# Output weights by column halves, and the tail of the first ring of expert chunks reordered

## The reference, cut to what matters

```python
x = x + merged @ w['w_out']                       # 1024 x 1024
hn = rms_norm(x, w['norm_ffn_g'])
x = x + hier_moe(hn, ...)                         # 4 groups of 8 experts, top 1 group, top 2 experts

def expert_block(xb, e):                          # D_EXPERT = 512, all float32
    return (silu(xb @ w_gate[e]) * (xb @ w_up[e])) @ w_down[e]
```

## Time and profile before

| | |
|---|---|
| median of 3 runs | 1033.21 us (1033.18 to 1034.37) |
| profiled execution | 1037.51 us |
| its span in the trace | 1035.7 us |
| TensorE busy | 903.2 us, 87% |
| VectorE, ScalarE, POOL busy | 365.3, 224.0, 85.9 us |
| SP queue (q1) | 244.93 MB, 59.4% of the 16 DMA engines' span |
| POOL queue (q0) | 12.89 MB, 4.7% |

### The profile page before, as it was taken

One profiled execution on the slowest core, in us unless ns is written; L12 is line 12 of the kernel. 1 busy time (PEld: TensorE's weight loads), 2 busy tenths in 40 slices (PEclk: granted clock), 3 DMA queues, 4 the chain that ended last, 5 costly groups with the idle time before them and its releaser, 6 DMA issues.

```text
span 1035.7 us, 11180 instructions
## 1 busy us (share of the span) xinstructions
PE 903.2 (87%) x4299; PEld 507.1 (49%) x4299; DVE 365.3 (35%) x806; ACT 224.0 (22%) x570; POOL 85.9 (8%) x89
## 2 busy tenths in 40 slices
PE   6899799999899999999859999787877788778784
PEld 5454677777678888755423433232332333233331
DVE  4588568767353345534414111111110101111010
ACT  3432354364622100032201111000010100001010
POOL 0100000000000000000011122010111011010111
PEclk9999899999999999999959999989999999999998
DMA  8622212112112228096369999999999999999991
GB/s 309 205 82 85 77 41 84 46 42 82 41 41 81 82 82 275 1 396 284 125 250 405 389 395 394 388 415 395 404 398 406 407 401 408 402 413 397 411 395 47
DMA packets 34095, 258.46 MB, mean 250 GB/s; under 512 B 9000, under 2 KB 12328, under 8 KB 18792
## 3 DMA queue, kind: packets, MB, share of 16 engines
q1 hardware_dynamic: 28000, 244.93, 59.4%
q0 software_dynamic: 6048, 12.89, 4.7%
HBM read 252.46 MB, written 14.58 MB: 258 GB/s over the span
## 4 chain that ended last, share of the span: by engine, by line
PE 55%; DMA 26%; DVE 7%; issue 6%; ACT 4%; SPq 1%; another core or an unknown queue 1%; POOL 0%; POOLq 0%; DVEq 0%; ACTq 0%
DMA arena<-in_w_gu 19%; PE ps L1723 19%; PE ps L1996 12%; PE ps L2015 7%; PE ps L1662 6%; DMA arena<-in_w_ed 5%; PE ps L1880 4%; PE ps L1985 2%; DVE arena L1289 1%; ACT arena L825 1%; DVE a_stat L1315 1%; DMA arena<-in_x_T 1%; DVE arena L1312 1%; DMA hn_rows<-arena 1%; ACT arena L837 1%
## 5 line engine op out<-in xcount | busy, mean ns | idle before, releaser
L1723 PE MATMUL ps<-arena 128*128 128x272 f32 x1120 | 269.4, 397 | 13.4 <-ACT arena L725 5.8
L1996 PE MATMUL ps<-arena 128*64 128x512 f32 x512 | 232.8, 603 | 19.7 <-DMA arena<-in_w_gu 19.5
L1723 PEld LDWEIGHTS ps<-arena 128*128 128x128 f32 x1120 | 209.9, 191 | 65.1 <-ACT arena L725 11.5
L1997 PE MATMUL ps<-arena 128*64 128x512 f32 x512 | 233.0, 603 | 0.0
L2015 PE MATMUL ps<-arena 128*64 128x512 f32 x512 | 134.6, 673 | 57.2 <-issue 44.0
L725 ACT ACTIVATE arena<-ps 128x272 f32<-128x272 f32 (+5 forms) x172 | 77.2, 457 | 401.5 <-PE ps L2015 175.3
L1996 PEld LDWEIGHTS ps<-arena 128*64 128x64 f32 x512 | 67.0, 138 | 156.1 <-issue 123.8
L1521 DVE SCALAR_TENSOR_TENSOR arena<-ps,list_w,arena 64x512 f32<-64x512 f32 x32 | 23.8, 743 | 286.5 <-ACT arena L990 286.5
L2015 PEld LDWEIGHTS ps<-arena 128*64 128x64 f32 x512 | 43.7, 153 | 145.8 <-issue 137.0
L1662 PE MATMUL ps<-arena 128*128 128x512 f32 (+1 forms) x192 | 75.6, 552 | 8.1 <-DMA arena<-in_w_kv 7.1
L685 POOL DMA_INDIRECT out_y<-arena,list_i x32 | 45.6, 1426 | 402.9 <-PE ps L1985 342.7
(11 more groups left out here) (224 smaller groups left out, 692.1 us busy)
## 6 DMA issues: line engine op xcount, KB each, us to landing
arena<-in_w_gu SPq DMA_DIRECT2D x64, 2048.0 KB, 48.6
arena<-in_w_ed SPq DMA_DIRECT2D x32, 2048.0 KB, 51.2
arena<-in_w_pair SPq DMA_DIRECT2D x20, 1024.0 KB, 4.8
arena<-in_x SPq DMA_DIRECT2D x8, 512.0 KB, 8.2
arena<-in_w_q SPq DMA_DIRECT2D x2, 2048.0 KB, 16.5
arena<-in_w_out SPq DMA_DIRECT2D x2, 2048.0 KB, 13.4
arena<-in_x_T SPq DMA_DIRECT2D x4, 512.0 KB, 8.9
out_y<-arena SPq DMA_DIRECT2D x4, 512.0 KB, 7.0
```

Source lines behind the costliest of these rows:

```text
L1723: ins = mm(out, w[:, k, :], tokens[:, k, :], start=k == 0 and q in "127", stop=k == 3, skip_group_check=q not in "127")
L1996: mm(ps[0:C, 2 + s, :], xT[s][:, j, :], w[:, jj, 0, :], start=j == 0, stop=j == JX - 1)
L1997: ins = mm(ps[64:64 + C, 2 + s, :], xT[s][:, j, :], w[:, jj, 1, :], start=j == 0, stop=j == JX - 1)
```

## The change

`w_out` is stored in HBM, and lies in the arena, by column halves: half c holds columns 512c to 512c + 511 of all rows, and takes 4096 words. Each is one transfer. The products read the same numbers in the same order.

SP's order in the output stage: after the y writes of tiles j = 1 to 3 it waits for `out_ready` 8 (half 0 of the last tile is multiplied, half 0 of `w_out` is free) and issues chunk 7 into words 0 to 4095. Then comes the y write of the last tile. Then SP waits for the last tile's normalised rows and writes them to `hn_rows` itself, with a semaphore of its own, `hn_last`; POOL no longer does. Then chunk 8. Then SP waits for `x_full[0]`, the landing of the first gathered rows, and issues chunk 9. Everything after that is as before. POOL's wait ahead of the first gather is changed to match.

```diff
-        w_out = area(0, KD, D)
+        w_out = [area(4096 * c, KD, 512) for c in range(2)]
@@
+        hn_last = sem("hn_last")
@@
             for kk in range(2):
-                sp.dma_start(w_out[:, 4 * kk:4 * kk + 4, :], k_major(a["w_out"])[:, 4 * kk:4 * kk + 4, :])\
-                  .then_inc(wo_in, 16)
+                sp.dma_start(w_out[kk], a["w_out"][kk]).then_inc(wo_in, 16)
@@
-            for j in range(1, NT):
+            for j in range(1, NT - 1):
                 start_y(j)
-            for n in range(EARLY, N_CHUNK):
-                load_chunk(n)
+            sp.wait_ge(out_ready, half_no(NT - 1, 0) + 1)
+            load_chunk(EARLY)
+            start_y(NT - 1)
+            sp.wait_ge(hn_ready, NT)
+            t = ORDER[NT - 1]
+            sp.dma_start(hn_rows[t * P:t * P + ROWS[t], :], xn[(NT - 1) % 2][0:ROWS[t], :]).then_inc(hn_last, 16)
+            load_chunk(EARLY + 1)
+            sp.wait_ge(x_full[0], 16)
+            load_chunk(EARLY + 2)
@@
-            for j, t in enumerate(ORDER):
+            for j, t in enumerate(ORDER[:NT - 1]):
                 pool.wait_ge(hn_ready, j + 1)
@@
-            pool.wait_ge(hn_out[0], 48)
+            pool.wait_ge(hn_out[0], 32)
             pool.wait_ge(hn_out[1], 32)
+            pool.wait_ge(hn_last, 16)
@@
-                        ins = mm(ps[DEC * q:DEC * (q + 1), 0, 0:D // 4], merged[:, k, SEQ:], w_out[:, k, q * 256:(q + 1) * 256],
+                        ins = mm(ps[DEC * q:DEC * (q + 1), 0, 0:D // 4], merged[:, k, SEQ:], w_out[q // 2][:, k, q % 2 * 256:(q % 2 + 1) * 256],
@@
-                    ins = mm(ps[:, 2 * (j % 2) + c, :], merged[:, k, t * P:(t + 1) * P], w_out[:, k, c * 512:(c + 1) * 512],
+                    ins = mm(ps[:, 2 * (j % 2) + c, :], merged[:, k, t * P:(t + 1) * P], w_out[c][:, k, :],
@@
-        "w_out": f(w_out)[0], "g_ffn": ...
+        "w_out": f(w_out)[0].reshape(KD, P, 2, 512).transpose(2, 1, 0, 3), "g_ffn": ...
```

More of the change, by code:

```diff
@@ L2081 @@
         "w_mix": f(pool_mix_w).reshape(KD, P, 256).transpose(1, 0, 2).reshape(P, KD * 256), "p_scale": f(pool_scale).reshape(KD, P).T,
-        "w_out": f(w_out)[0], "g_ffn": np.stack([f(norm_ffn_g)[0].reshape(KD, P).T, f(norm_ffn_g)[0].reshape(P, JX)], axis=1),
+        "w_out": f(w_out)[0].reshape(KD, P, 2, 512).transpose(2, 1, 0, 3), "g_ffn": np.stack([f(norm_ffn_g)[0].reshape(KD, P).T, f(norm_ffn_g)[0].reshape(P, JX)], axis=1),
         "w_group": f(w_route_group)[0], "b_group": f(b_route_group)[0],
```

## The result

| | before | after |
|---|---|---|
| timed beside each other | 1034.9 us (7 runs) | 1028.84 us (1027.32 to 1031.04, 7 runs) |
| ratio after / before | | 0.9945, 95% interval 0.9928 to 0.9962 |
| profiled execution | 1037.51 | 1030.08 |
| span | 1035.7 | 1028.2 |

The change makes the kernel faster, by 5.7 us by the ratio of these runs. The forecast was 1024.6 us, 8.6 us less, with a range up to 1028.5; the measured median lies just above it, and the saving is smaller than forecast. One of the runs of before took 1310 us and is not among those compared.

The account below looks back on a forecast made before the run. Chunk 10's issue plus fixed traffic was taken as the bound. Gather start 4.9 plus landing 4.3 gave 9.2 us, cut to 8.6; chunk 7, chunk 9, w_out and clock 0; off 1033.21 gives 1024.6 us, range 1022.9 to 1028.5.

Parts of the forecast that it names:

- The bound: Whole kernel: the end is chunk 10's issue plus fixed traffic; time saved before that issue comes off the end.
- Chunk 7: Output stage: issued at 501.32 instead of 511.44, landed by 508.9 ahead of the last tile's second half; cost 0, saving alone 0.
- The row write: Last tile's rows, written by SP ahead of chunk 8: landing in 4.9 us, at 518.9; ends 516.9 and 524.6.
- First gather: POOL's first gather of rows, after rows_listed at 519.76: starts at 520.6, 4.9 us earlier.
- Landings: First two gathers: 3.3 us each, the first instead of 7.6, gaining 4.3 us; ends 2.9 and 11.9.
- first expert matmul: TensorE, after turns from 524.3: at 526.6 instead of 535.21, 8.6 us earlier, capped by weight list and second rows.
- Chunk 9: Behind the first rows: issued at 524.0, landing in 7.6 us, off the engines at 531.3 before chunk 10's 532.0; cost 0.
- The clock: TensorE's rise to 2.4 GHz near the first expert products: counted as 0, with 1.7 us possible either way.
- A late clock: First expert products: clock rises later, 1.7 us less gain, 1026.3 us; inside the range, no chance of its own.
- I take it off the median as it is: Final sum: the 8.6 us saving subtracted from the earlier median 1033.21 us, though the profiled execution stood 4.3 us above it.
- the mechanism's rivals: Slow second rows 1028.5 us (0.14), clock rising early 1022.9 (0.04), no gain 1032.8 (0.05), chunk 9 overtaking the rows 1043.1 (0.03).
- The rival of the slow rows: Second gather beside chunks takes 7.6 us, first expert matmul at 530.5, gain only 4.7 us, 1028.5 us; chance 0.14.

Follow-up runs that it names:

- e10: Changed kernel with chunk 8 too issued only after the first gathered rows land, so chunks 8 and 9 follow them; 1033.65 us, ratio 0.9959 to the kernel before.
- e2: Changed kernel with chunk 9 issued right behind chunk 8, without the wait for the first rows; 1032.39 us, ratio 0.9951 to the kernel before.
- e3: Changed kernel with chunk 7 issued behind the last row write, just ahead of chunk 8, not early; 1032.05 us, ratio 0.9959 to the kernel before.
- e6: Changed kernel with chunk 9 released by a POOL semaphore behind the first two gathers, not by the first rows' landing; 1033.58 us, ratio 0.9976 to the kernel before.
- e1: Changed kernel timed again without any edit, beside the kernel before; 1027.38 us, ratio 0.9908.
- e11: Changed kernel timed a third time without any edit, beside the kernel before; 1028.6 us, ratio 0.9922.
- e12: Kernel before with only output weights by halves and chunk 7 early; row write on POOL, chunk 9 without wait; 1033.4 us, ratio 0.9954 to the kernel before.
- e5: Changed kernel with 20 unread products on TensorE just ahead of the first turn of gathered rows; 1044.5 us, ratio 1.0083 to the kernel before.
- e8: Changed kernel with 16 unread products in TensorE's waits and chunk 9 released by POOL's semaphore behind the first gathers; 1036.54 us, ratio 1.0002 to the kernel before.
- e4: Changed kernel with the last row write back on POOL, so chunk 8 is queued ahead of it; 1031.74 us, ratio 0.9955 to the kernel before.

## Why the prediction was right and where it was wrong

**The bound: right.** The end follows the issue of chunk 10. In 14 profiles of 12 kernels, whose chunk 10 goes out between 21.5 and 38.7 us after the last y write, the rest of the span is 494.3 to 496.6 us, with e10 the only exception; and medians less that moment are 1005.8 to 1007.9 us. Differences under some 2 us lie within that scatter. That it is the stream of chunks, and not TensorE, is shown by e10.

**The steps, one by one.** Chunk 7 at 501.17 (forecast 501), landed in 7.4 us. That is not "ahead of the last tile's second half", as the forecast had it, but during it: the second half was multiplied from 502.30 to 509.82. The chunk disturbed nothing, for the eight products beside it took 3.63 us as in the earlier trace rows.

```profile
502.30 3.63 PE ps L1888 x8
```

The row write at 513.68, landed in 2.9 us: the lower end, where 4.9 was taken; without effect, since rows_listed was late next, as said. First gather 520.66 (forecast 520.6). Landings 3.9 and 3.1 us (forecast 3.3 each). Turns 524.71 (524.3), first expert matmul 526.67 (526.6), so 8.54 us gained where 8.6 was forecast. Chunk 9 at about 524.6 (524.0), landed in 8.7. That is 533.3 and later than chunk 10's issue, but its packets were through by 532, and chunk 10 landed in 7.3 us, as quickly as the 7.6 of the earlier trace rows.

**The clock: a term of the sum that was put at 0.** The first half of gate and up took 5.97 us (526.67 to 532.64) instead of 5.38, because the clock rose some 4.5 us after the first expert matmul, not 3.4. TensorE had worked since 521.51 with hardly a gap, where before it had stood for 9 us. So chunk 10 gained 7.95 us, 0.6 less than the matmul. A late clock stood in the forecast with up to 1.7 us; that part of it came. Whether this belongs to the kernel or to the run isn't shown: the three profiles of the changed kernel have 5.97, 5.93 and 5.87 us for this half, and other kernels, with other pauses of TensorE before it, 5.52 (e2), 5.41 (e3) and 4.86 us (e6).

**The step that failed: "I take it off the median as it is".** The measured median is 4.2 us above the forecast. The clock accounts for 0.6 of them, the base for 3.4. The median of before was that of three runs, 1033.21 us. It was no fair base. In the later sessions the same kernel had 1036.33, 1036.62 and 1037.3 us over 61 runs, none below 1033.6, on three chips that hardly differ in it. The profile had shown it: the profiled execution took 1037.51 us, and I noted that it stood 4.3 us above the median and left it there. By the table, 1033.21 less 29.53 is 1003.7, three microseconds below every other remainder. From 1036.6 the forecast would have been 1028.0, against 1028.84, 1027.38 and 1028.6 measured. The range had no term for this scatter. Its upper end held the mechanism's rivals only, and the measured median is 0.3 us outside it.

What scatters lies ahead of all that was changed. The profiles reach the last y write at 507.8 to 511.1 us. Most of this is there by 42 us: the same 16 matmuls of the first projection took 8.57 us in before, 8.56 in after and 6.87 in e3, by the clock they were granted (mean 0.92 in 22 to 44 us in the first two, 1.00 in e3). The chains, of before, after and e3:

```profile
32.53 8.57 PE ps L1662 x16
```

```profile
32.85 8.56 PE ps L1670 x16
```

```profile
31.73 6.87 PE ps L1669 x16
```

The 14 profiles fall into two groups here: 8.27 to 8.57 us in seven (before, after, e1, e2, e10, e11, e12) and 6.87 us in the other seven, though every edit of this document lies behind that point in TensorE's work. The Trainium skill, "TensorE: Matmul & The Clock Gate", Part 1, says that the moment at which the clock changes isn't tied to the kernel's start and moves from run to run. These profiles agree with it. The medians of the two groups don't differ once chunk 10's moment is taken off (1005.9 to 1007.9 and 1005.8 to 1007.5 us, e10 aside), so it goes with the single run and not with the kernel.

Of the 3.2 us between the last y writes of before (511.06) and e5 (507.82), 1.0 lies ahead of these matmuls (they start at 32.53 and 31.55), 1.7 in them, and 0.6 between 65 and 439 us, where the first output product starts at 438.92 and 435.68. Why the first three runs of before were quick was not settled; no profile of one of them exists. And the first comparison's 5.7 us is in part the same thing: three of its seven runs of before are those.

**The rival of the slow rows.** It was priced with 7.6 us for a gather beside chunks. e2, e3, e6 and e8 show 7.5 to 9.4. It did not come true because chunk 8 left the engines in time, at 521 to 522 us as reckoned, and both of the change's chunk moves were needed for that: e2 and e3, each with one of them undone, lose 4.6 and 4.3 us.

**What each part is worth.** Undone alone, in the issue of chunk 10: chunk 9's wait 4.6 us, chunk 7 early 4.3, the write on SP 4.0; together 12.9, more than the 7.9 of the whole. Done alone, chunk 7 early brings 4.0 (e12). They don't add, because each takes away one of two waits: the write (10 us behind a chunk, 3 ahead of it) or the gather (8 us beside a chunk, 4 in an empty queue). With the write late the queue has emptied by the time of the gather, so one wait hides the other. The output weights by halves, whose only use is to free chunk 7's slot, were not undone alone. The traces show no cost of theirs: the load took 12.5 us (before 13.4), and the first output product started at 438.84 (before 438.92).

## To carry to other kernels

When a stage is bound by a stream of transfers, look for the one event that starts the steady stream, and count whatever delays it at full price (17.2 us of delay cost 17.1 in e5). Ahead of that event a bulk transfer should not lie in front of or beside a small one that the path waits for; here each such place cost 4 to 5 us. It is cheapest behind the small one, as long as it is through before the stream starts. And take an absolute time off the distribution of the base, not off three runs: where the profiled execution stands 4 us above the median, one of the two is not typical, and the range has to hold both.

## What was not expected of the hardware

- A transfer from POOL's queue that met a chunk in SP's queue took long however much lay there: the row write took 9.9, 10.7 and 10.6 us behind one, two and three chunks of 2 MB (e4, e12, before), and 2.9 alone. The Trainium skill, "DMA: Bandwidth & Descriptors", Queues, rings and completion order, says that a DMA engine alternates between its queues packet by packet. The trace agrees with it only once q0 runs: in e6 both queues have packets in 523 to 526 us, but q0's first came some 4 us after the gather's start, against 1 to 2 us in the changed kernel. The same late start, 3 to 4 us, is in before, e2, e4 and e12. What holds it back at first was not found. In e4 there was a late end too: 0.49 of the write's 0.5 MB had moved by 518 us, and a few last packets of both queues came until it landed at 521.0; chunk 8 took 12.0 us there.
- Sixteen turns of gathered rows (64x64) take 2.0 us at either clock: 2.00 at 1.2 GHz in the changed kernel, 1.98 at 2.4 GHz in e5. The matmuls of 512 columns behind them halve: one every 0.85 us there, one every 0.43 us here.
- A semaphore that POOL raises behind two indirect DMAs in its program had let SP go on 0.34 us after the start of the first, which takes 1 us (e6). It doesn't say that they are issued.
